# Hybrid decoder step on eight cores: V projected in token layout, longer background work, and norm squares added up before one ones product

## What is computed

```
x += 0.5 * SwiGLU(RMSNorm(x))                     # FFN 1, d_ff 2816
h  = RMSNorm(x); z = h @ w_in
A: 12 attention units (4 heads x 3 groups: window, dilation = (128,1), (512,4), (2048,16));
   query t reads keys t, t-d, ..., t-window; outputs k and v of the last `window` positions
B: HGRN2 recurrence, 4 heads;  C: cross attention into 256 memory tokens
merged = gates * branches @ w_o;  x += merged
x += 0.5 * SwiGLU(RMSNorm(x)); y = RMSNorm(x)     # FFN 2, final norm
rmsnorm(x) = x * rsqrt(mean(x*x over 1024 channels) + eps) * g
```

## Time and profile before

| | |
|---|---|
| median of 3 runs | 1920.72 us (1918.43 to 1957.67) |
| the profiled execution | 1921.48 us, span 1919.7 us |
| TensorE busy | 1795.8 us, 94% |
| DVE busy | 753.8 us, 39% |
| ScalarE busy | 665.1 us, 35% |
| POOL busy | 108.3 us, 6% |

### The profile page before, as it was taken

How to read it: one execution, slowest core, us unless ns; L and a number is a source line. 1 busy time by engine, 2 the same in 40 slices (tenths; PEclk the granted TensorE clock), 3 DMA queues, 4 the chain that set the end, 5 groups by cost and what they waited for, 6 DMA issues and landing times.

```text
span 1919.7 us, 31734 instructions; the slowest of 8 cores (1910.7 to 1919.7 us)
## 1 busy us (share of the span) xinstructions
PE 1795.8 (94%) x11055; PEld 1022.7 (53%) x11055; DVE 753.8 (39%) x1469; ACT 665.1 (35%) x1305; POOL 108.3 (6%) x212
## 2 busy tenths in 40 slices
PE   5999999999999989889879689999999999999995
PEld 2555555555555555555545445555555555555553
DVE  2332111322356667668535444444562221113322
ACT  3441100332266576576335432222342111003321
POOL 2000000100000000000000100000000000000001
PEclk8999999999999999999889889999999999999998
DMA  9688536954632416126223574343234877846563
GB/s 196 130 158 152 125 61 152 168 98 80 136 62 64 71 30 121 20 51 129 67 67 79 86 192 102 64 93 65 57 101 89 165 158 137 152 84 137 123 115 96
DMA packets 48586, 203.23 MB, mean 106 GB/s; under 512 B 7600, under 2 KB 16432, under 8 KB 42288
## 3 DMA queue, kind: packets, MB, share of 16 engines
q0 software_dynamic: 25632, 108.01, 35.3%
q1 hardware_dynamic: 22800, 93.20, 16.4%
HBM read 278.93 MB, written 74.24 MB: 184 GB/s over the span
## 4 chain that ended last, share of the span: by engine, by line
PE 85%; ACT 5%; DVE 4%; issue 3%; DMA 2%; POOL 0%; ACTq 0%; DVEq 0%; POOLq 0%; SPq 0%
PE ps L426 32%; PE ps L449 16%; PE ps L600 12%; PE ps L1146 9%; PE ps L1149 4%; PE ps L689 2%; PE ps L327 2%; PE ps L749 2%; PE ps L654 1%; PE ps L1212 1%; ACT bfr L324 1%; DMA R<-x_t 1%; PE ps L1010 1%; PE ps L640 1%; DMA pmk<-R 1%
## 5 line engine op out<-in xcount | busy, mean ns | idle before, releaser
L426 PE MATMUL ps<-hT,WB 128*128 128x416 bf16 (+1 forms) x3520 | 625.1, 338 | 6.5 <-DVE hT L339 6.5
L426 PEld LDWEIGHTS ps<-hT,WB 128*128 128x128 bf16 x3520 | 344.9, 98 | 277.9 <-issue 13.4
L449 PE MATMUL ps<-R,WB 128*128 128x416 bf16 (+1 forms) x1760 | 310.4, 337 | 0.0
L440 ACT ACTIVATE f32r<-ps 128x416 f32<-128x416 f32 (+1 forms) x220 | 112.3, 513 | 567.0 <-PE ps L426 537.9
L441 DVE TENSOR_TENSOR R<-ps,f32r 128x416 bf16<-128x416 f32 (+1 forms) x220 | 128.8, 585 | 435.5 <-PE ps L426 314.2
L600 PE MATMUL ps<-hT,WB 128*128 128x416 bf16 (+1 forms) x1320 | 253.3, 343 | 4.1 <-DVE R L617 3.2
L449 PEld LDWEIGHTS ps<-R,WB 128*128 128x128 bf16 x1760 | 172.2, 98 | 133.2
L1146 PE MATMUL ps<-hT,WB 128*128 128x416 bf16 (+1 forms) x960 | 188.9, 340 | 1.5 <-ACT R L1152 1.5
L600 PEld LDWEIGHTS ps<-hT,WB 128*128 128x128 bf16 x1320 | 126.6, 99 | 103.7 <-issue 13.0
L324 ACT ACTIVATE bfr<-R 128x416 bf16<-128x416 f32 (+4 forms) x185 | 98.0, 542 | 196.7 <-DVE R L455 107.7
L455 DVE SCALAR_TENSOR_TENSOR R<-ps,R 128x416 f32<-128x416 f32 x80 | 46.8, 585 | 255.6 <-PE ps L449 191.8
(11 more groups left out here) (192 smaller groups left out, 1535.1 us busy)
## 6 DMA issues: line engine op xcount, KB each, us to landing
WB<-w1gu POOLq DMA_DIRECT2D x44, 512.0 KB, 9.8
WB<-w2gu POOLq DMA_DIRECT2D x44, 512.0 KB, 7.3
sw2v<-cw2v SPq DMA_DIRECT2D x60, 256.0 KB, 6.6
sw2k<-cw2k SPq DMA_DIRECT2D x60, 256.0 KB, 6.3
WB<-w1d POOLq DMA_DIRECT2D x16, 704.0 KB, 7.1
WB<-w2d POOLq DMA_DIRECT2D x16, 704.0 KB, 7.7
WB<-w_mrg POOLq DMA_DIRECT2D x8, 1152.0 KB, 11.3
WB<-w_att POOLq DMA_DIRECT2D x11, 768.0 KB, 9.0
```

The source lines that it names most:

```text
L426: P.op(PE, lambda e: e.matmul(p_.t[:, :n], lhsT=wv[:, c, j2 * 128:(j2 + 1) * 128], rhs=hT[:, c, t0:t0 + n], start=(c == 0), stop=(c == 7)) ...
L440: P.op(ACT, lambda e, sg=sg, pg=pg: e.activation(out=sg.t[:, :n], in_=pg.t[:, :n], func=AF.Silu), reads=[pg.d], writes=[sg.d])
L449: P.op(PE, lambda e, j=j: e.matmul(pd.t[:, :n], lhsT=dv[:, j, :], rhs=act[:, j, si * 416:si * 416 + n], start=(j == 0), stop=(j == NJ - 1) ...
```

## The change

Three parts.

**The norms' squares.** A class `Sq_sum` takes the place of `Prog_sq` and of the loop in `norm_gen`. Where it is given an f32 buffer, the square of chunk 0 goes there, those of chunks 1 to 6 are added to it one by one on DVE (on POOL in the output projection), the add of chunk 7 writes bf16, and one product with ones follows. The first three norms of FFN 1 have no such buffer and keep their eight products. The buffers `accs0` and `accs1` lie in parts of R2 that are free at the time.

**V.** q and k stay; v is computed with a 128-token tile of `hT` (tokens with the stride of the dilation) as the weights and the 128 columns of `w_v` as the moving operand, 16 tiles by 8 chunks, and a product for the 4 sample tokens. The transposes go; `v_sink` copies four tiles at a time and stores the window through a ring of two buffers. A projection has 15 steps in place of 19.

**Order.** `bg` takes a third step in every fifth pair; `att_sample` starts after 8 steps in place of 4, and what is left of it may run within `merge`; the memory K/V outputs have 4 staging buffers; the first merge weights are loaded ahead of `kvg`, the second at pair 92.

```diff
+    class Sq_sum:
+        def __init__(self, ti, accb=None, eng=DVE):
+            self.ti, self.pb, self.todo, self.acc, self.eng, self.n = ti, psN.next(), [], accb, eng, G[ti]
+        def chunk(self, c, d_src):
+            src, n = xv(self.ti)[:, c, :], self.n
+            sb = self.acc if self.acc is not None and c == 0 else bfr.next()
+            P.op(ACT, lambda e: e.activation(out=sb.t[:, :n], in_=src, func=AF.Square, scale=1.0 / 32), reads=[d_src], writes=[sb.d])
+            self.todo.append((c, sb))
+            if len(self.todo) > 1:
+                self.one()
+        def one(self):
+            c, sb = self.todo.pop(0)
+            n, pb, ac = self.n, self.pb, self.acc
+            if ac is not None and c == 0:
+                return
+            if ac is not None and c < 7:
+                P.op(self.eng, lambda e: e.tensor_tensor(out=ac.t[:, :n], in0=ac.t[:, :n], in1=sb.t[:, :n], op=ALU.add), reads=[sb.d, ac.d], writes=[ac.d])
+                return
+            if ac is not None:
+                s2 = sb
+                P.op(self.eng, lambda e: e.tensor_tensor(out=s2.t[:, :n], in0=ac.t[:, :n], in1=s2.t[:, :n], op=ALU.add), reads=[s2.d, ac.d], writes=[s2.d])
+            first = c == 0 or ac is not None
+            P.op(PE, lambda e: e.matmul(pb.t[:, :n], lhsT=ones_b, rhs=sb.t[:, :n], start=first, stop=(c == 7)), reads=[sb.d, d_one], writes=[pb.d])
+    def norm_gen(ti, gcol, dst_of, done=None, accb=None):
+        sq = Sq_sum(ti, accb)
         for c in range(8):
+            sq.chunk(c, dxh[ti][c // 4] if ti < 3 and gcol is gf1 else dx[ti])
             yield
+        sq.flush()
+        yield
+        yield from norm_rest(ti, gcol, dst_of, sq.pb, done)
...
-            for kidx in range(3):
+            for kidx in range(2):
...
         for q4 in range(4):
+            pb = psA.next()
+            for i in range(4):
+                r, b = divmod(q4 * 4 + i, nb)
+                t0 = r + dil * 128 * b
+                for c in range(8):
+                    P.op(PE, lambda e, c=c, pb=pb, i=i, t0=t0: e.matmul(pb.t[:, i * 128:(i + 1) * 128], lhsT=hT[:, c, t0:t0 + dil * 127 + 1:dil], rhs=w3[:, 2, c, :],
+                                                                        start=(c == 0), stop=(c == 7)),
+                         reads=[wb.d] + rd[c], writes=[pb.d])
+            v_sink(A_, s, g, q4, pb)
+            yield
...
+        cp(A_["v"][:, q4 * 4:q4 * 4 + 4, :], pb.t[:, :].rearrange("p (i n) -> p i n", i=4), [pb.d], [A_["dv"]])
+        if g == 0 and q4 < 3:
+            return
+        lo = 0 if g == 2 else 384
+        sb = vst_r.next()
+        cp(sb.t[:, lo:512], pb.t[:, lo:512], [pb.d], [sb.d])
...
-    mst_r = Ring([Buf(r1a(73088 + i * 2048, 2048, F32)) for i in range(2)])
+    mst_r = Ring([Buf(r1a(o, 2048, F32)) for o in (73088, 75136, 60800, 62848)])
...
-            sq = Prog_sq(ti, 2)
+            sq = Sq_sum(ti, accs0[ti % 2], POOL)
...
+                    pre_m.append(load_mrg(0))
                     for i in range(8):
                         load_kvg(i)
-                    bg = chain(delay(4), att_sample())
-            if gp == 90:
-                pre_m.append(load_mrg(0))
+                    bg = chain(delay(8), att_sample())
+            if gp == 92:
+                pre_m.append(load_mrg(1))
...
             for k in range(2):
                 next(bg, None)
-                while nproj * 14 < 19 * (2 * p + k + 1) and nproj < 19:
+                if k == 0 and gp % 5 == 4:
+                    next(bg, None)
+                while nproj * 14 < 15 * (2 * p + k + 1) and nproj < 15:
                     next(proj, None)
...
-        run(bg)
         run(fins)
+        return bg
```

127 lines of the change are left out of this document (66 added, 61 removed).

## The result

| | before | after |
|---|---|---|
| median of the runs compared | 1920.7 us | 1975.8 us (lowest 1965.9) |
| profiled execution | 1921.5 us | 1967.1 us |
| ratio of comparable executions, 95% interval | | 1.027 (1.019 to 1.036) |

The changed kernel is slower by 2.7%; the forecast was 1917 us.

The account below looks back on a forecast made before the run. TensorE was taken to bound the first FFN, a DVE and ScalarE chain the output projection. Norms +17 and mixer -21 took 1921.5 us to 1917; range 1885 to 1952.

Parts of the forecast that it names:

- The third step: Mixer: background 13 steps ahead, drain empty at unit 11, its waits at L1034 gone, -6.4 us.
- Loads in the last unit: Mixer's end: both merge weights and twelve kvg take 37 us at 145 GB/s, +9 us (+3 to +14).
- The staging buffers' -3.8: Mixer: with four memory K/V buffers, ScalarE and TensorE no longer wait for the `pmk` store, -3.8 us.
- Half clock: Mixer: with shorter waits, one or two stretches at the 1.2 GHz level go, -3 us.
- The rival of slow V: V matmuls: unhidden weight loads add 42 ns each; 1938 us (stride 16 only, 0.12) or 1982 (all units, 0.08); chance 0.20.
- The forecast for V and its relief: Mixer: TensorE -2 us, no wait for the last v copy -8.5, ScalarE and DVE relief -6 (bounds 0 and 17).
- The norms: FFNs, output projection, mixer's start, tail: -1.8 + 8 + 7 + 3.9 = +17 us.
- the rival in which the waits don't come: Norms and mixer: adds early enough, norms -14.6 us, mixer up to 35; 1872, mostly 1880 to 1895; chance 0.17.
- The mixer's start: TensorE waits 0.6 us at the first flush, about 4 at group 4's product, 2 before its q: +7 (+3 to +10).
- The output projection: DVE's chain sets 13.6 us a group; POOL's last add and half clock at the boundaries cost +8 us (+1 to +17).
- The tail: Kernel's end: group 4's last add stands behind norm 3's applies, +3.9 us.
- The rival "POOL's adds hold DVE": Apply phases: each POOL add delays one DVE instruction 0.5 to 1.06 us; 8 to 17 us, 1925 to 1934; chance 0.10.

Follow-up runs that it names:

- `kvg_late`: The kernel before, with the eight kvg loads also waiting for the last write of the memory attention: 1935.5 us, ratio 1.009.
- `no_third_step`: The changed kernel without the third background step in every fifth pair: 1931.8 us.
- `v_norms`: The kernel before plus V in token layout and the norms' squares added up, without third step or new order, two staging buffers: 1914.2 us, ratio 0.997.
- `third_mem`: The kernel before with twelve extra background steps, all in the memory-attention part (even pairs 64 to 86): 1944.8 us, one execution.
- `burst8`: The kernel before with eight extra background steps at one place, pair 13 in unit 1: 1950.1 us, ratio 1.015.
- `v_early`: The kernel before plus V and norms' sums on DVE, last add right behind chunk 7's square, eight products in the output projection: 1889.6 us, ratio 0.984.
- `v_pool`: The kernel before plus V and norms' sums, `norm_gen` and `sqs` adds on POOL, eight products in output projection and `fsq`: 1969.2 us, ratio 1.028.

## Why the prediction was wrong, point by point

**The third step: the step that failed.** The prediction said: "Its work is spread, its waits (6.4 us at L1034) go: -6.4. With the shorter waits one or two half-clock stretches like the earlier trace rows go: -3." The drain did become empty and L1034 did stop waiting. But the price of a step was taken as nothing wherever it lands. Alone it cost 46.6 us in the mixer, 27.6 of them idle and 19.0 lost to the lower clock. Counted by place, units 0 to 10 took 64.7 us more, for the 31 us of work and waits that left unit 11's column (54.9 less the 23.7 of the earlier trace rows): some 33 us lost in the pairs. The last unit itself took some 12 us more than its 23.7, the kvg loads that `kvg_late` reproduced with 14.3. On top of V the step cost 35 us (1967.1 against 1931.8). The prediction also never asked what "13 steps ahead" does to a pipeline whose period is two pairs. Why the pairs lose time stays open; the runs show where it is lost and that it goes with the place of `hg_pair`'s starts.

**Loads in the last unit.** Forecast +9 with a last unit of 33 us; measured 44.6. The loads were priced as if they left when unit 11's projection ended, "some 6 us before that unit begins"; they left 11.8 us after its start (1111.84), behind the window store that V's staging ring had put in front of them, and in the traces before, the drain hid them. The sum priced bandwidth; what the runs show is a queue. Without the third step the new order still costs 10.8 us at the end of the mixer (79.8 against 69.0 in unit 11 with its drain) and 4.1 in the merge (258.4 against 254.3), into which half clock runs (0.73 from 1110 to 1130 in `no_third_step`, in `v_norms` none): 18 us by the profiled executions of the two, 14 by medians over the executions that the ratios use. 12 of it are TensorE's waits for `kvg`, which stood behind merge weights whose buffer was in use. The staging buffers' -3.8 can't be seen in it.

**Half clock.** -3 was expected. In the changed kernel's mixer 101 us ran at 1.2 GHz, against 59 before. On core 7 the clock fell ten times there, each time behind idle pieces of 1.0 to 4.4 us, alone or several in a row. Counting the idle time alone misses two fifths of what the third step cost. Of the prediction's last sign of being wrong, half-clock stretches through the output projection, two short ones came (6.8 us from 1432.6, 3.4 us from 1466.7).

**V: right in kind, size under-estimated.** The rival of slow V did not come. Two runs of 64 and 64 matmuls without another between, V of a unit with stride 1 and of one with stride 16:

```profile
819.15 3.74 PE L634 MATMUL ps<-WB,hT 128*128 128x128 bf16 x64
```

```profile
1092.48 4.15 PE L634 MATMUL ps<-WB,hT 128*128 128x128 bf16 x64
```

Starts lie 56 ns apart at strides 1 and 4 and 62 ns at stride 16, against the 57 taken. By that the strided units lose 512 x 0.006 = 3 us, not 21. The Trainium skill (TensorE: Matmul & The Clock Gate, Back-to-back issue gap) gives 81 ns for sustained 128-column matmuls; this trace doesn't agree. The Trainium skill's rule on strided bf16 reads (SBUF — State Buffer, The DMA port swizzle) has the right sign at stride 16, and the price here is 6 ns. The forecast for V and its relief was -2 - 8.5 - 6 = -16.5; measured -20 in the mixer (583.1 against 603.1). What part each term had was not measured.

**The norms: right, the total smaller.** Forecast +17, measured +13 (1914.2 against 1901.3); so the rival in which the waits don't come fell. One product is miswritten in the prediction: 42 x 0.175 + 7 x 0.165 is 8.5; eight groups make 56 products less, 49 x 0.175 + 7 x 0.165 = 9.7, and that is what the 9.8 stands for. Gate/up: the forecast's 1.55 us of waiting against 1.38 to 1.48. One of the changed kernel's products in FFN 1:

```profile
355.53 0.34 PE L379 MATMUL ps<-bfr,cbf 128*128 128x416 bf16 x1 [1.45 <-DVE bfr L377]
```

The mixer's start: +7 forecast. The first flush waited 0.5 us as said, the second product 3.3, but the 2 us more before the q of group 4 came out as 0.2. The start took 36.6 us against V alone's 33.5, the mixer as a whole 5.3 more (588.4 against 583.1).

```profile
517.75 0.45 PE L379 MATMUL ps<-bfr,cbf 128*128 128x388 bf16 x1 [3.32 <-DVE bfr L377]
```

The output projection: +8 forecast, +5.3 measured (72.8 against 67.5). The waits at the four boundary products are 1.6, 4.9, 2.7 and 4.1 us, and the period is 16.5 us where 15 was expected. Its chain is the one foreseen, DVE still held 0.85 us by the square, and POOL's last add in front of the product:

```profile
1425.44 1.28 POOL L373 TENSOR_TENSOR R<-R,bfr 128x416 f32<-128x416 f32 x1 [0.57 <-ACT bfr L362]
...
1429.08 0.59 DVE L1265 TENSOR_TENSOR R<-ps,R 128x416 f32<-128x416 f32 x1 [0.85 <-ACT bfr L362]
...
1433.52 0.97 POOL L377 TENSOR_TENSOR bfr<-R,bfr 128x416 bf16<-128x416 f32 x1 [0.47 <-ACT bfr L362]
...
1434.63 0.50 PE L379 MATMUL ps<-bfr,cbf 128*128 128x416 bf16 x1 [4.91 <-POOL bfr L377]
```

The tail: +3.9 forecast, the add stands behind the applies as said, and FFN 2 with the tail took 2.8 us more than with eight products (487.7 against 484.9).

```profile
1950.85 0.56 DVE L377 TENSOR_TENSOR bfr<-R,bfr 128x388 bf16<-128x388 f32 x1
...
1951.55 0.48 PE L379 MATMUL ps<-bfr,cbf 128*128 128x388 bf16 x1 [9.15 <-DVE bfr L377]
```

The rival "POOL's adds hold DVE" did not come at its price. Both engines were slowed beside each other, but a pair of applies took 1.42 us instead of 1.22, two pairs a group, where 0.5 to 1.06 us was assumed for each of four adds.

**The parts together.** By the profiled executions, each part against the kernel without it: V -20, norms +13, order, loads and buffers +18, third step +35. They give the 46 us by the way they are made, so the sum is no test of them; by medians over the executions that the ratios use they are -18, +12, +14 and +38. The forecast had the first two within 4 us each and the other two, +5 and -9, short by 57.

**Open.** Whether the place of `hg_pair`'s start alone makes the idle time; a kernel with one extra step at the start of the mixer and none after it would tell. Where a step in the memory part of the background loses its time (`third_mem`, and units 8 to 10 of `burst8`), since it has no such phase. What the longer delay of the sample attention has in the few microseconds of the order's cost that are not waits for `kvg`.

## What to carry to other kernels

Before work is moved out of a drain, ask what the drain covers: here loads that could not start earlier, 12 to 14 us. A load put first on a queue holds all behind it for as long as its buffer is in use (12 us here). Where a generator with a fixed period is woven into a loop with another, count the steps modulo the period; one extra step shifts everything behind it (that this is what costs here is read from the traces, not tested). An operation that a later product needs goes right behind its input in the program, ahead of what would queue in front of it (`v_early`, for the norms' last add), and not on the queue that issues the weights (`v_pool`). Where a step inside the pairs can go without cost, these runs don't show.

## What the runs showed of the hardware

128-column matmuls with fresh weights each took 56 ns from start to start in runs of 64 at full clock, and 62 ns when the weights were read with a stride of 16 bf16 elements (changed kernel, core 7, 1536 matmuls). A POOL add of 128x416 f32 took 0.97 us alone and 1.28 us beside two-input applies of DVE; the pair of applies took 1.42 us instead of 1.22. Both engines were slowed, neither was shut out, and the rule that such instructions contend (the Trainium skill, SBUF — State Buffer, Who interferes with whom) is borne out with that price.
